# Carrying the inverse roots of three inner RMS norms to all partitions through a row in DRAM

## What is computed

```
def rmsnorm(x, g):
    y = xf * lax.rsqrt(jnp.mean(xf * xf, axis=-1, keepdims=True) + EPS)
    return (y * g.astype(jnp.float32)).astype(x.dtype)
def swiglu(h, w_gate, w_up, w_down):
    return (jax.nn.silu(h @ w_gate) * (h @ w_up)) @ w_down
...
x = x + 0.5 * swiglu(rmsnorm(x, ffn1_norm[l]), ...)
h = rmsnorm(x, mix_norm[l]); proj = h @ w_in[l]
...                      (mLSTM heads and pooled groups from proj)
x = x + mix
x = x + 0.5 * swiglu(rmsnorm(x, ffn2_norm[l]), ...)
return rmsnorm(x, final_norm)
```

## Time and profile before

| | |
|---|---|
| median of 3 executions | 914.16 us (914.05 to 914.57) |
| the profiled execution | 913.21 us |
| its span in the profile | 911.2 us |
| TensorE (PE) busy | 895.9 us, 98% of the span |
| VectorE (DVE) busy | 681.1 us, 75% |
| ScalarE (ACT) busy | 456.3 us, 50% |
| DMA, share of 16 engines | about 30% |
| granted TensorE clock, mean | 0.995 of full speed |

### The profile page before, as it was taken

One profiled execution on the slowest core, in us unless ns is written; L12 is line 12 of the kernel. 1 busy time (PEld: TensorE's weight loads), 2 busy tenths in 40 slices (PEclk: granted clock), 3 DMA queues, 4 the chain that ended last, 5 costly groups with the idle time before them and its releaser, 6 DMA issues.

```text
span 911.2 us, 15640 instructions
## 1 busy us (share of the span) xinstructions
PE 895.9 (98%) x5598; PEld 809.2 (89%) x5598; DVE 681.1 (75%) x1176; ACT 456.3 (50%) x752; POOL 43.6 (5%) x64
## 2 busy tenths in 40 slices
PE   8999999999999999999999999999999999999995
PEld 6899999999988888888888788999999999888885
DVE  7899999999543434677887679799999998534334
ACT  7565566666422323544872465566666665323220
POOL 0000000000000000001534100000000000000001
PEclk9999999999999999999999999999999999999997
DMA  6233333332432323222212232233323332433212
GB/s 242 73 114 112 96 103 104 111 96 69 173 116 93 115 92 116 70 92 70 70 47 73 90 116 70 94 102 106 107 100 102 105 110 86 141 103 116 93 47 92
DMA packets 38996, 91.73 MB, mean 101 GB/s; under 512 B 4288, under 2 KB 6464, under 8 KB 38960
## 3 DMA queue, kind: packets, MB, share of 16 engines
q1 hardware_dynamic: 38640, 90.72, 30.1%
q0 software_dynamic: 176, 0.46, 0.2%
q10 hardware_dynamic: 144, 0.08, 0.0%
HBM read 89.14 MB, written 2.10 MB: 100 GB/s over the span
## 4 chain that ended last, share of the span: by engine, by line
PE 91%; DVE 5%; DMA 2%; issue 1%; ACT 1%; POOL 0%; DVEq 0%; SPq 0%; ACTq 0%
PE ps L357 16%; PE ps L359 16%; PE ps L358 16%; PE ps L463 13%; PE ps L465 13%; PE ps L464 13%; DVE w_lo L1337 1%; PE ps L409 1%; DMA mask<-consts 1%; PE ps L387 1%; PE ps L393 1%; PE ps L390 1%; DMA raw<-weights 1%; PE ps L630 0%; DMA x<-x_t 0%
## 5 line engine op out<-in xcount | busy, mean ns | idle before, releaser
L1220 DVE TENSOR_TENSOR w_lo<-raw,w_hi 128x1024 fp32r<-128x1024 f32 x84 | 104.3, 1242 | 121.0 <-ACT w_hi L783 115.5
L357 PE MATMUL ps<-act_hi,w_hi 128*128 128x512 f32 (+1 forms) x470 | 178.9, 381 | 0.2 <-DVE act_lo L1692 0.2
L358 PE MATMUL ps<-act_lo,w_hi 128*128 128x512 f32 (+1 forms) x470 | 178.2, 379 | 0.0
L359 PE MATMUL ps<-act_hi,w_lo 128*128 128x512 f32 (+1 forms) x470 | 178.2, 379 | 0.0
L463 PE MATMUL ps<-xg_hi,w_hi 128*128 128x256 f32 x608 | 174.8, 288 | 1.4 <-DVE work L1373 1.4
L465 PE MATMUL ps<-xg_hi,w_lo 128*128 128x256 f32 x608 | 172.1, 283 | 0.0
L464 PE MATMUL ps<-xg_lo,w_hi 128*128 128x256 f32 x608 | 171.8, 283 | 0.0
L783 ACT ACTIVATE w_hi<-raw 128x1024 fp32r<-128x1024 f32 x76 | 80.2, 1056 | 157.6 <-PE ps L359 155.0
L463 PE MATMUL ps<-xe_hi,w_hi 128*128 128x256 f32 x456 | 128.0, 281 | 0.0
L465 PE MATMUL ps<-xe_hi,w_lo 128*128 128x256 f32 x456 | 127.2, 279 | 0.0
L464 PE MATMUL ps<-xe_lo,w_hi 128*128 128x256 f32 x456 | 127.2, 279 | 0.0
(11 more groups left out here) (205 smaller groups left out, 1404.9 us busy)
## 6 DMA issues: line engine op xcount, KB each, us to landing
raw<-weights SPq DMA_DIRECT2D x85, 512.0 KB, 3.3
raw<-weights SPq DMA_DIRECT2D x152, 256.0 KB, 2.6
x<-x_t SPq DMA_DIRECT2D x8, 256.0 KB, 6.8
first<-weights SPq DMA_DIRECT2D x8, 256.0 KB, 5.9
out<-x SPq DMA_DIRECT2D x6, 256.0 KB, 2.3
out<-x SPq DMA_DIRECT2D x4, 128.0 KB, 2.3
arena<-pool_w POOLq DMA_DIRECT2D x1, 256.0 KB, 2.9
vec<-vecs ACTq DMA_DIRECT2D x1, 73.5 KB, 3.1
```

Of the source, the lines that this page charges most:

```text
L357: pe.matmul(acc, hi, m_hi, start=first, stop=False)
L358: pe.matmul(acc, hi, m_lo, start=False, stop=False)
L359: return pe.matmul(acc, lo, m_hi, start=False, stop=last)
L1220: dve.tensor_tensor(w_lo[:, k % SLOTS], raw[:, k % RAWS], f32(w_hi[:, k % SLOTS]), ALU.subtract).then_inc(lo_made, 1)
```

## The change

The products with the identity and DVE's copy are taken out for stages 0, 1 and 2. In their place SP issues two transfers: it waits for the last step of `rsqrt`, writes `ycol` (128 partitions x 4 numbers) to one row of 512 numbers in a scratch tensor in DRAM, waits until that has landed, and reads the row back onto all 128 partitions of `rinv`. DVE waits for the second transfer where it waited for PE. The two transfers stand in SP's list behind the loads 4 and 5 (stage 0), between the loads MIX+5 and MIX+6 (stage 1), and behind the first four block loads of the second FFN (stage 2). In DVE's list some instructions are put ahead of the wait: in stage 0 the low part of unit 5, in the mixer the low part of unit MIX+4, in stage 2 the low parts of factors 1 and 5. PE's wait before product 2 of a first period is now for the read of `ps_rep` by the first step of `inverse_rms`.

```
+            def spread_rinv(stage):
+
+                sp.wait_ge(col_step, STEPS * (stage + 1))
+                sp.dma_start(rows[stage].rearrange("(b p) -> p b", p=P), ycol[:], allow_slow_non_contiguous=True
+                             ).then_inc(row_out, 16)
+                sp.wait_ge(row_out, 16 * (stage + 1))
+                sp.dma_start(rinv[:], rows[stage:stage + 1].partition_broadcast(P)).then_inc(rinv_in, 16)
...
                 load_block(p, 0, 2)
                 load_block(p, 0, 3)
+                if p == 1:
+                    spread_rinv(2)
                 with sp.Fori(1, NSP[p]) as s:
...
+            spread_rinv(0)
             units(SLOTS + RAWS, DN1)
             strassen_blocks(0)
-            units(DN1 + RAWS, DN2)
+            units(DN1 + RAWS, MIX + 6)
+            spread_rinv(1)
+            units(MIX + 6, DN2)
             strassen_blocks(1)
...
-            def replicate(stage):
-
-                pe.wait_ge(col_step, STEPS * (stage + 1))
-                spread_columns(ps_rep, range(TB)).then_inc(rep_made, 1)
-
...
                     if head:
-                        pe.wait_ge(rinv_made, stage + 1)
+                        pe.wait_ge(col_step, STEPS * stage + 1)
...
             def take_rinv(stage):
-                dve.wait_ge(rep_made, stage + 1)
-                dve.tensor_copy(rinv[:], ps_rep).then_inc(rinv_made, 1)
-                dve.wait_ge(rinv_made, stage + 1)
+                dve.wait_ge(rinv_in, 16 * (stage + 1))
...
                     terms_lo(0, 1)
+                    split_lo(5, 5)
                     take_rinv(stage)
                     plain_gate(0)
-                    split_lo(5, 5)
                     plain_product(0)
...
                 sum_2(0)
+                lo_of(1, 0, 0)
+                lo_of(5, 0, 0)
                 if p == 1:
                     take_rinv(stage)
                     plain_gate(0)
-                lo_of(1, 0, 0)
-                lo_of(5, 0, 0)
-                if p == 1:
                     plain_product(0)
...
                 inverse_rms(1)
+                split_next()
                 take_rinv(1)
...
                 gates_in()
-                split_next()
```

More of the change, by code:

```diff
@@ L99, with build_layer @@
 S_COLS = 1280
-def build_layer(nc, weights, pool_w, x_t, vecs, consts, out):
+def build_layer(nc, weights, pool_w, x_t, vecs, consts, rows, out):
     ctx = ExitStack()
@@ L198, in build_layer @@
         sq_made, ssq_made, ssq_zero = sem("sq_made"), sem("ssq_made"), sem("ssq_zero")
-        ms_made, rep_made, rinv_made = sem("ms_made"), sem("rep_made"), sem("rinv_made")
+        ms_made, rep_made = sem("ms_made"), sem("rep_made")
+        row_out, rinv_in = sem("row_out"), sem("rinv_in")
         col_step = sem("col_step")
@@ L419, in mean_columns, with ffn_up @@
                 mm.then_inc(ms_made, 1)
-            def replicate(stage):
-                pe.wait_ge(col_step, STEPS * (stage + 1))
-                spread_columns(ps_rep, range(TB)).then_inc(rep_made, 1)
-            def ffn_up(base, p, stage, mean_at, rep_at):
+            def ffn_up(base, p, stage, mean_at):
                 def plain(f):
@@ L434, in hook @@
                                 mean_columns(stage)
-                            if (unit, k) == rep_at:
-                                replicate(stage)
                         return hook
@@ L684, in mixer @@
                         column_block(n, n, ps[:, qk_bank[i % 3]])
-                        if i == 0:
-                            replicate(1)
                         continue
@@ L764, in _ @@
             pe.wait_ge(vec_in, 16)
-            ffn_up(UPP1, 0, 0, None, (4, 1))
+            ffn_up(UPP1, 0, 0, None)
             ffn_down(DN1, 0, 0, KD // 4)
             mixer()
-            ffn_up(UPP2, 1, 2, (1, 2), (2, 0))
+            ffn_up(UPP2, 1, 2, (1, 2))
             ffn_down(DN2, 1, 2, KD // 4 - 1)
@@ L1764, in last_block @@
                     inverse_rms(3 + a, slice(2 * a, 2 * a + 2))
-                    dve.wait_ge(rep_made, 4 + a)
+                    dve.wait_ge(rep_made, 1 + a)
                     if a == 0:
@@ L1872 @@
     out = nc.dram_tensor("out", (D, T), F32, kind="ExternalOutput").ap()
-    build_layer(nc, *args, out)
+    rows = nc.dram_tensor("rows", (3, T), F32, kind="Internal").ap()
+    build_layer(nc, *args, rows, out)
     r = run_bass_kernel_spmd(nc, [arrays], core_ids=[0])
```

## The result

The changed kernel takes **938.25 us** (median of 6 runs, 936.86 to 939.66), the kernel before 914.08 in the same comparison (6 runs): a ratio of 1.0271, 95% interval 1.0259 to 1.0283. It is slower by 24 us, where +2.2 us was forecast and 920.4 was the upper end. The profiled execution took 937.88 us, with a span of 936.1. PE's busy time grew by 5 us, the span by 24.9; the rest is idle time of PE.

What follows compares the result with a forecast made beforehand. DVE's queue was taken to bound stage 0 up to 73.37 us and the later part of stage 2, PE stage 1. The terms 2.4 - 0.9 + 0.7 = +2.2 on 914.16 gave 916.4 us, range 913.8 to 920.4.

Steps and rivals of the forecast that it cites:

- the size of the write: First transfer, ycol to DRAM, 512 packets of 4 bytes: 3.0 us, ends 2.3 and 5.0.
- The read: Second transfer, DRAM row to all partitions of rinv, 256 KB in 2-KB rows like a block load: 2.6 us.
- L: Time from the last rsqrt step's end to DVE's first read of rinv: 6.0 us, range 5.0 to 8.0.
- The page's rule: Skill's small-packet rate for the write, about 10.5 ns a packet: about 6.8 us in all, sum about +9.8; set aside.
- rival B: Both transfers short, L from 5.0 to 5.4: no change, between 914.4 and 915.2 us; chance 0.22.
- Stage 0, L - 3.58: Delay of `terms` in stage 0 through DVE's queue, carried to PE's stall at 73.37: +2.4 us.
- Stage 1, -0.9: Stage 1, the mixer: wait covered by a low part, nothing later, PE keeps the removed matmuls' time: -0.9 us.
- Stage 2, L - 5.29: Delay of `sum_1` in stage 2, waiting for block 3's load, passed on to PE: +0.7 us.
- The removal, 0.9 us a stage: Four identity products gone from PE each stage: 0.89 us a stage, 2.67 for three, whole gain if PE bounds everywhere.
- Rival C: Write of single numbers slow, 5.0 us, L = 8.0: 920.4 us, slower; chance 0.15.
- A: PE is the bound everywhere, DVE's delays vanish: 911.5 us, faster; chance 0.08.
- Q: Theory formed after the result: transfers hold up SP's queue, weight loads come late, each stage harms the next; no chance.

Runs made afterwards that it cites:

- e11: The change without the write and its wait, reading 128 input rows into rinv, values left out: 911.24 us against 913.94 for the kernel before, ratio 0.9968.
- the first three runs: The kernel before with the DRAM round trip in one stage only: stage 0 923.18 us (ratio 1.0117), stage 1 919.92 (1.0075), stage 2 920.54 (1.0084).
- e12: Kernel before with the round trip in stage 1 alone, 16-byte write packets, rinv read straight, values left out: 913.53 us, ratio 0.9997.
- e6: The change with another write and read form each stage, values left out; writes: 16-byte packets 1.4 us, 8-byte packets 1.4, 512 packets 64 bytes apart 1.9.
- e5: The change with other transfer forms, SP waiting for each read; writes: 512 packets 64 bytes apart 2.85 us, 128 packets 16 bytes apart 1.4, change's form 8.29.
- e9: The change with another write form each stage, SP waiting for reads; 128 16-byte packets 1.4 us, 512 4-byte packets at 8 bytes 3.4 in two orders.
- e8: Kernel before with the round trip in stage 1 alone, 16-byte write packets, DVE reading rinv with a step of four: 917.59 us, ratio 1.0046.

## Why the prediction was wrong, point by point

- **The failed step is the size of the write.** "So I take 0.03 us a packet and 3.0 us", with 5.0 as the upper end: measured 8.0 (8.0 to 10.2 over all kernels with this form). The upper end came from the average packet of the trace, which is 2.3 KB, the lower from the 128-KB store, which I called "four times the row size of mine": it has rows of 1 KB, and the write has packets of 4 bytes. No row of before shows many small packets side by side in DRAM, and that, not the count, goes with the price. An upper end from the nearest row was no upper end.
- **The read** was taken as a block load, 2.6: measured 5.0 (4.8 to 5.9), the second mis-sized term, 2.4 us a stage. As the two trade against each other, the firm figure is their sum, 13.0 to 13.9 instead of 5.6. With it L left its range of 5.0 to 8.0, one of the signs named for being wrong.
- **The page's rule.** The 5.4 us plus latency, about 6.8, that I worked out from the Trainium skill, "DMA: Bandwidth & Descriptors", section "Bandwidth", came closer than my 3.0. That figure was measured on transfers issued from GpSimd, and so was the fit of 2.0 us plus bytes that rival B cites; the ones here are issued from SP. Its mechanism is not what the runs show: 512 packets took 1.9 to 3.4 us when spread out, and 128 side by side took 7.0. I let the trace's average of 7.1 ns overrule it; that average holds for other packets.
- **Stage 0, L - 3.58.** With L = 14.0 it gives +10.4. `terms` starts 49.87 - 30.09 = 19.78 us after the stage's first row instead of 9.38: +10.4. "PE is as far behind as DVE" held too: PE reaches the Strassen period at 84.69, 10.6 behind once the start-up's 0.8 is taken off. The stall for unit 6 is the one I had named for an L 2 us longer.
- **Stage 1, -0.9.** Right only as long as the cover lasts. The first scaled projection was to come 0.4 us earlier than before at L = 6.0, so at 13.1 it is 6.7 late: measured (392.16 - 375.45) - (373.86 - 363.87) = 6.7. That "nothing is later" rested on L, and with it gone the stage costs 6.2: stalls of 5.0, some 2 of half clock (12 matmuls from 442 to 446 where 22 go at full clock), less the 0.9. "Nothing is later" is the second step that failed, and only because of the first. I had no price for the clock, since nothing in the rows of before falls below 1.00 there.
- **Stage 2, L - 5.29.** +7.7 at L = 13.0; `sum_1` is (602.69 - 577.32) - (577.23 - 559.53) = 7.7 later, waiting for the block load as described, and the stage lost 7.1.
- **The removal, 0.9 us a stage,** is borne out only for stage 1, which is 1.0 us shorter in e11. That e11 gains 2.9 us in all doesn't tell 3 x 0.89 = 2.7 from the working, which gave -2.5 with the saved matmuls of stages 0 and 2 lost in the stalls.
- **Rival C** had the right mechanism, but its 5.0 us for the write was bounded by the same row. **A** fails on DVE's idle waits of 8.7 to 11.8 us that PE follows; **B** on both sizes. Q, formed only after the result, fell with the first three runs.

No version that computes the whole result beats the kernel before. With 16-byte packets the round trip in stages 0 and 2 still loses 4.7 us, because two transfers of 1.4 to 2.6 and 3.4 to 5.2 us cannot match the 3.2 and 3.8 us of the matmuls and the copy. e12, whose tokens stand in the wrong order, shows what the mixer would lose and gain if the row came in the right order with such a write: nothing that can be told from none.

## What to carry to other kernels

Before a small result is sent through DRAM, look at where its packets land: have each partition write its numbers as one packet (change the order in which they are computed, if need be), or leave a gap between them, and time the write by itself before planning on it. When a duration has no row, an average over other packets bounds nothing; work out what each stage would cost at two or three times the duration, and see which cover ends there. Every wait that left PE idle for 3.1 us or more here had half clock behind it, and of fifteen between 2.3 and 2.8 us seven had; such a wait is to be priced with 1 to 4 us more than its own length.

## What the runs showed that I had not expected

- 4-byte packets to DRAM without a gap, 16 in 64 bytes: 7.0 us for 128 of them, 8.0 to 10.2 for 512; 512 of them with 8, 4 or 1 in 64 bytes 3.4, 2.8 and 1.9 to 2.8.
- A write of that form and the read of its row took 13.0 to 14.1 us together in seven round trips, while the write alone ranged over 2.2 us and the read over 2.8.
- A row read back onto 128 partitions right behind its write took 4.2 and 4.8 us, an old or an input row onto all partitions 3.0 to 3.7, each with nothing behind it in the queue.
- A DVE multiplication of 128x512 fp32 numbers takes 1.05 us instead of 0.68 when its SBUF operand is read with a step of four. The Trainium skill, "SBUF — State Buffer", section "Door 1: The DMA port swizzle (why `[64,N]` ≈ `[32,N]`)", says that SBUF is read in lines of 16 bytes and that each access to a new line costs more; with four fp32 numbers a step is one such line, and the run agrees with that: 1048 ns against 680. The same note gives four fp32 numbers as how far one can stride for free, and that the run contradicts. Other steps were not tried.
- The granted clock of PE was 0.50 (1.2 GHz) behind every stall of 3.1 to 7.0 us in the fourteen traces, for 2 to 8 us of work, which cost 1 to 4 us. Behind stalls near 2.5 us it was so in some and not in others: behind the same stall of 2.46 us for the last plain gate it was 0.50 in the changed kernel and e6, and 1.00 in e5 and e9. Behind shorter ones in the body of the kernel it stayed at 1.00, but for 0.52 in e8, 2 us behind a stall of 0.93.
